# First loads of a decoder-layer kernel in another order, a separate buffer for the sample tokens, and query products in two groups of 64 columns

## The reference

```
mod = c @ w_ada + b_ada;  shift, scale, gate = split(mod, 3)
h = rmsnorm(x, g_norm) * (1 + scale) + shift
u = h @ w_in                       # queries, six k/v parts, gate logits, z_a, latents, z_b
y = [ NSA group * silu(z_a) | MLA group * silu(z_b) ]
x = x + gate * (y @ w_out);  then a final rmsnorm
```

## Time and profile before

| | |
|---|---|
| runs of the kernel before | 1237.3, 1240.06, 1241.99 us; median 1240.06 |
| the profiled execution | 1236.88 us |
| its span in the trace | 1235.1 us |
| mean granted clock of TensorE | 0.976 of full |
| busy: PE, DVE, ACT, POOL | 93%, 44%, 26%, 7% |
| first pass over the weights ends (L498 starts) | 231.9 us |

### The profile page before, as it was taken

How to read it: one execution, slowest core, us unless ns; L and a number is a source line. 1 busy time by engine, 2 the same in 40 slices (tenths; PEclk the granted TensorE clock), 3 DMA queues, 4 the chain that set the end, 5 groups by cost and what they waited for, 6 DMA issues and landing times.

```text
span 1235.1 us, 20092 instructions
## 1 busy us (share of the span) xinstructions
PE 1153.9 (93%) x7510; PEld 784.9 (64%) x7510; DVE 546.7 (44%) x1421; ACT 317.8 (26%) x636; POOL 86.6 (7%) x209
## 2 busy tenths in 40 slices
PE   6498999899999999998999999999999799999997
PEld 3265767544454667786878786865444466666665
DVE  0111211111111357776656564542333477777774
ACT  1111211110111256555434343431111122222220
POOL 0000000000000012111000000000000200000000
PEclk9698999999999999999999999999999899999997
DMA  9836220200000341000000000001982287666670
GB/s 344 221 111 226 61 94 9 88 7 4 6 4 7 69 111 51 2 1 1 1 1 2 1 2 1 2 1 67 169 285 71 84 294 249 228 224 224 214 198 20
DMA packets 91703, 115.89 MB, mean 94 GB/s; under 512 B 38513, under 2 KB 61476, under 8 KB 90584
## 3 DMA queue, kind: packets, MB, share of 16 engines
q1 hardware_dynamic: 91608, 114.61, 29.9%
HBM read 102.31 MB, written 12.27 MB: 93 GB/s over the span
## 4 chain that ended last, share of the span: by engine, by line
PE 74%; issue 9%; DVE 6%; ACT 5%; SPq 4%; DMA 2%; POOL 0%; ACTq 0%; POOLq 0%; DVEq 0%
PE PS L507 13%; PE PS L1583 9%; PE PS L1305 8%; PE PS L1336 6%; PE PS L1286 6%; PE PS L459 4%; PE PS L484 4%; ACT AR L1356 4%; PE PS L1275 3%; PE PS L1974 3%; PE PS L474 2%; PE PS L1939 2%; DMA AR<-in_x_prompt 2%; PE PS L1987 2%; PE PS L1282 2%
## 5 line engine op out<-in xcount | busy, mean ns | idle before, releaser
L1305 PE MATMUL PS<-AR 128*128 128x65 f32 (+1 forms) x1344 | 173.3, 269 | 0.9 <-DVE AR L1476 0.9
L1305 PEld LDWEIGHTS PS<-AR 128*128 128x128 f32 x1344 | 165.0, 192 | 1.3 <-issue 1.3
L507 PE MATMUL PS<-AR 128*128 128x512 f32 (+1 forms) x384 | 159.6, 575 | 2.7 <-DVE AR L755 2.7
L1356 ACT ACTIVATE AR<-PS,SM_ 128x64 f32<-128x64 f32 (+8 forms) x224 | 121.3, 594 | 54.4 <-PE PS L1336 36.2
L507 PEld LDWEIGHTS PS<-AR 128*128 128x128 f32 x384 | 72.3, 190 | 84.9 <-issue 81.2
L1336 PE MATMUL PS<-CA,AR 128*128 128x128 f32 x704 | 115.8, 280 | 0.2 <-ACT AR L1356 0.2
L1583 PE MATMUL PS<-AR 128*128 128x512 f32 x256 | 111.7, 592 | 0.0
L1393 DVE TENSOR_REDUCE SM_<-PS 128x2 f32<-128x512 f32 (+6 forms) x62 | 58.9, 950 | 114.3 <-PE PS L1286 62.3
L1336 PEld LDWEIGHTS PS<-CA,AR 128*128 128x128 f32 x704 | 80.3, 148 | 30.2 <-issue 15.6
L1366 ACT ACTIVATE AR<-PS 128x512 f32<-128x512 f32 (+1 forms) x108 | 59.1, 547 | 152.6 <-PE PS L1336 152.0
L1286 PE MATMUL PS<-AR 64*128 64x128 f32 (+3 forms) x512 | 74.3, 409 | 10.8 <-ACT AR L1356 10.2
(11 more groups left out here) (337 smaller groups left out, 1358.5 us busy)
## 6 DMA issues: line engine op xcount, KB each, us to landing
AR<-in_cache_nsa SPq DMA_DIRECT2D x128, 256.0 KB, 5.1
AR<-in_cache_mla SPq DMA_DIRECT2D x128, 96.0 KB, 4.2
AR<-in_x_prompt SPq DMA_DIRECT2D x16, 512.0 KB, 5.0
AR<-in_w_ada SPq DMA_DIRECT2D x3, 2048.0 KB, 15.7
AR<-in_w_in SPq DMA_DIRECT2D x1, 5888.0 KB, 17.7
out<-AR SPq DMA_DIRECT2D x9, 512.0 KB, 3.0
AR<-in_w_ada SPq DMA_DIRECT2D x8, 512.0 KB, 4.0
AR<-in_w_out SPq DMA_DIRECT2D x4, 1024.0 KB, 9.7
```

The lines of the kernel that those rows point to most:

```text
L507: mm = pe.matmul(PS[0:n, bank, 0:hi - lo], ht(j, k)[:, 0:n], w2cols(k, lo, hi), start=(k == 0), stop=(k == KT - 1))
L1305: mm = pe.matmul(out, tile, v, start=(n == 0), stop=(n == nb - 1))
L1356: act.activation(PB[:, o:o + n], PSF[:, o:o + n], ACT.Exp, bias=NM[:, u % 2, gi:gi + 1], scale=-1.0).then_inc(s_exp, 1)
```

## The change

It does five things.

1. The sample tokens get a buffer of their own (`XSS`), so `XS[0]` and `XS[1]` hold prompt tiles 1 and 2, tile j+2 goes into the buffer of tile j only for j from 1 to 6, and the loads have three semaphores.
2. SP's first loads stand in another order: `w_ada` as three loads of two k and two of one k, four of the six bias rows, tile 1, `W1` columns 512 to 1303 in one load, the query weights in one load, tile 2, the relative-bias table, the first two `ADAG`. The two last bias rows, three constant tables and the page table are loaded in round 1, after x of tile 3. In round 0 SP issues no x load.
3. The query weights are loaded as they lie in memory, 2 KB per row (before: 16 loads that reorder heads, 256 bytes a piece).
4. The prompt queries are products of 64 weight columns, group 0 to PSUM partitions 0 to 63 and group 1 to 64 to 127: twice as many products as before, each with the same 128 tokens. The sample queries read the same columns as the moving operand in two runs of 64.
5. In PE's rounds A comes first, and the transposes of tile j+1 and the gate pair stand behind A (in round 1 behind the sample queries and sample keys too). The transposes of tile 0 stand ahead of step 6 of the modulation, whose result goes to bank 7. ACT and DVE square and scale tile 2 at the end of round 0, behind the copies of the sample tokens' A and B.

```
@@ sp_projection
-            sp.dma_start(ADA[0], ada_v[:, 0, 0:2048]).then_inc(s_ada[0], 16)
...
-            for k in range(KT):
-                for g in range(G):
-                    sp.dma_start(W1[:, k, 0:512].rearrange("p (r g d) -> p r g d", r=R, g=G)[:, :, g, :],
-                                 w_in2[:, k, 256 * g:256 * g + 256].rearrange("p (r d) -> p r d", r=R))\
-                        .then_inc(s_w1q, 16)
...
+            sp.dma_start(XS[0], x_t[1]).then_inc(s_x[1], 16)
+            sp.dma_start(W1[:, :, 512:W1N], w_in2[:, :, 512:W1N]).then_inc(s_w1, 16)
+            sp.dma_start(W1[:, :, 0:512], w_in2[:, :, 0:512]).then_inc(s_w1q, 16)
+            sp.dma_start(XS[1], x_t[2]).then_inc(s_x[2], 16)
             sp.wait_ge(s_us, 1)
             sp.dma_start(U_dram, US[0:8, :]).then_inc(s_udma, 16)
             for j in IDX:
-                if j + 2 <= 8:
+                if 1 <= j <= 6:
                     sp.wait_ge(s_xt, j + 1)
-                    sp.dma_start(XS[j % 2], x_t[j + 2]).then_inc(s_x[j % 2], 16)
+                    sp.dma_start(xs(j + 2), x_t[j + 2]).then_inc(s_x[(j + 2) % 3], 16)
...
                 if j + 2 < KT:
                     sp.wait_ge(s_gk, 2 * j + 2)
@@ pe_projection
                 for r in range(R):
                     for k in range(KT):
-                        mm = pe.matmul(PS[:, 2, P * r:P * r + n], w1q(k, r), ht(j, k)[:, 0:n],
-                                       start=(k == 0), stop=(k == KT - 1))
+                        for g in range(G):
+                            mm = pe.matmul(PS[64 * g:64 * g + 64, 2, P * r:P * r + n], w1q(k, r, g), ht(j, k)[:, 0:n],
+                                           start=(k == 0), stop=(k == KT - 1))
```

More of the change, by code:

```diff
@@ L289, in ht, with xs @@
             return HTS[:, k, :] if j == 0 else HT[:, j - 1, k, :]
+        def xs(j):
+            return XSS if j == 0 else XS[(j - 1) % 2]
         def tok(j):
@@ L307, in z_mla, with w1q, w1q_both @@
             return ZNS[96:128, 0:512] if j == 0 else Z[:, j - 1, 512:1024]
-        def w1q(k, r):
-            return W1[:, k, P * r:P * r + P]
+        def w1q(k, r, g):
+            return W1[:, k, 256 * g + 64 * r:256 * g + 64 * r + 64]
+        def w1q_both(k, r):
+            return W1[:, k, 0:512].rearrange("p (g r d) -> p r g d", g=G, r=R)[:, r]
         def w2cols(k, lo, hi):
@@ L338, in sp_projection @@
-            sp.dma_start(W1[:, :, 512:1024], w_in2[:, :, 512:1024]).then_inc(s_w1, 16)
-            sp.dma_start(W1[:, :, 1024:W1N], w_in2[:, :, 1024:W1N]).then_inc(s_w1b, 16)
-            for k in range(KT):
-                for g in range(G):
-                    sp.dma_start(W1[:, k, 0:512].rearrange("p (r g d) -> p r g d", r=R, g=G)[:, :, g, :],
-                                 w_in2[:, k, 256 * g:256 * g + 256].rearrange("p (r d) -> p r d", r=R))\
-                        .then_inc(s_w1q, 16)
+            for n, base in enumerate((31360, 35456, 10432)):
+                sp.dma_start(view(base, 4096).rearrange("p (k n) -> p k n", k=2),
+                             ada_v[:, 2 * n:2 * n + 2, 0:2048]).then_inc(s_ada[n], 16)
+                if n == 0:
+                    sp.dma_start(RBA[0:32, :], rel_bias).then_inc(s_rb, 16)
+                    sp.dma_start(CB[0:33, :], cB).then_inc(s_rb, 16)
+                    sp.dma_start(GST[0:8, :], g_norm[0].rearrange("(k p) -> k p", p=P)).then_inc(s_rb, 16)
+                    sp.dma_start(GST[8:10, :], g_q_lat[0].rearrange("(k p) -> k p", p=P)).then_inc(s_rb, 16)
+                    sp.dma_start(XSS[0:RS, :], x_t[0]).then_inc(s_x[0], 16)
@@ new lines, in sp_projection @@
+            for k in (6, 7):
+                sp.dma_start(ADA[k], ada_v[:, k, 0:2048]).then_inc(s_ada[k - 3], 16)
+            for c in range(4):
+                sp.dma_start(BADA[32 * c:32 * c + 32, :], b_ada[:, 512 * c:512 * c + 512].to_broadcast([32, 512]))\
+                    .then_inc(s_bada, 16)
+            sp.dma_start(XS[0], x_t[1]).then_inc(s_x[1], 16)
+            sp.dma_start(W1[:, :, 512:W1N], w_in2[:, :, 512:W1N]).then_inc(s_w1, 16)
+            sp.dma_start(W1[:, :, 0:512], w_in2[:, :, 0:512]).then_inc(s_w1q, 16)
@@ new lines, in sp_projection @@
+                if j == 1:
+                    for c in (4, 5):
+                        sp.dma_start(BADG[32 * c - 128:32 * c - 96, :],
+                                     b_ada[:, 512 * c:512 * c + 512].to_broadcast([32, 512])).then_inc(s_bada, 16)
+                    sp.dma_start(CC[:], cC).then_inc(s_cst, 16)
+                    sp.dma_start(CD[:], cD).then_inc(s_cst, 16)
+                    sp.dma_start(CE[:], cE).then_inc(s_cst, 16)
+                    sp.dma_start(GKV, g_kv_lat.to_broadcast([P, P])).then_inc(s_cst, 16)
+                    sp.dma_start(PT_SB[:], page_table.rearrange("b n -> (b n)").rearrange("(a m) -> a m", a=1))\
+                        .then_inc(s_cst, 16)
@@ L411, in pe_projection @@
             for k in range(KT):
[L412 to L413 removed]
+                if k % 2 == 0 or k == 7:
+                    pe.wait_ge(s_ada[k // 2 if k < 6 else k - 3], 16)
+                if k == 6:
+                    pe.wait_ge(s_ctv, 4)
+                    pe_tokens(pe, 0)
                 for n in range(4):
[L415 removed]
+                    mm = pe.matmul(PS[32 * n:32 * n + 32, 7, :], CT[:, k, :], ADA[k][:, 512 * n:512 * n + 512],
                                    start=(k == 0), stop=(k == KT - 1))
@@ L452, in pe_projection @@
                     continue
[L453 to L456, removed]
                 pe.wait_ge(s_Ae, j)
@@ L470, in pe_projection @@
                     pe_keys(pe, 0)
+                if j < 8:
+                    pe_tokens(pe, j + 1)
+                pe.wait_ge(s_adag[(j - 1) % 2], 16 * ((j - 1) // 2 + 1))
+                for c in range(2):
+                    pe.matmul(PS[32 * c:32 * c + 32, 6, :], CT[:, j - 1, :], ADAG[(j - 1) % 2][:, 512 * c:512 * c + 512],
+                              start=(j == 1), stop=(j == KT)).then_inc(s_gk, 1)
                 pe.wait_ge(s_Be, j)
@@ L657, in act_squares @@
             junk = HT[0:n, (7, 6)[j] if j < 2 else j - 1, :, :].rearrange("p k t -> p (k t)")
-            act.activation(junk, XS[j % 2][0:n, :], ACT.Square, accum_out=SSQ[0:n, j:j + 1]).then_inc(s_ssq, 1)
+            act.activation(junk, xs(j)[0:n, :], ACT.Square, accum_out=SSQ[0:n, j:j + 1]).then_inc(s_ssq, 1)
         def dve_projection(dve):
```

54 lines of the change are left out of this document (18 added, 36 removed).

## The result

| | before | changed |
|---|---|---|
| median of ten runs each | 1239.85 us | 1250.97 us |
| lowest and highest | 1237.3, 1242.2 | 1245.1, 1256.3 |
| profiled execution (its span) | 1236.88 (1235.1) | 1246.68 (1244.9) |
| first pass over the weights ends | 231.9 | 239.3 |

The changed kernel is slower: 1.0085 of before, 95% interval 1.0069 to 1.0102. In a second set on another occasion it was 1.0101 (1.0086 to 1.0117). The forecast was 1248 (+8.1 us), the range 1242 to 1256.

What follows compares the result with a forecast made beforehand. PE, busy 93% of the span, was taken as the bound. Terms: +1.4 us to the keys of tile 2, +2.5 in round 3, +3.6 in round 4, +0.5 for Q, about +8.1: 1248 from a 1240.06 median; 8-in-10 range 1242 to 1256.

Steps and rivals of the forecast that it cites:

- the four waits: PE idle in rounds 1 to 4: 8.1 us at the sample queries, 12.4 before keys of tile 2, then 2.4 and 3.5.
- wait at the sample queries: Round 1: PE waits 8.1 us at the sample queries' transpose, until DVE has scaled tile 3 and copied them out.
- keys of tile 2: Round 2: keys start at 110.3 us, +1.4, behind `W2` and x of tile 4; PE stands 12.4 us instead of 5.4.
- wait before the keys of tile 3: Round 3: B and Q end 10.9 us behind the gate pair, DVE's copy 13.3 behind it: a stall of 2.4 us.
- wait before the keys of tile 4: Round 4: DVE's copy comes 14.4 us behind the gate pair, against 10.9 of B and Q: a stall of 3.5 us.
- Q in pairs, a round: Prompt queries as 128 products of 64 columns: 0 to 0.95 us more a tile, taken as 0.1, 0.5 in sum.
- Up to T1: Front to the end of round 1's gate pair: fed by memory, ending at 56.1 us, 6.9 earlier, bounds 55.0 to 58.
- The flights of x: Rounds 1 to 4: gate pair to release stays as before, 11.9, 23.3, 13.3 and 14.4 us for tiles 3 to 6.
- The early gain stays: Rival, 6%: x comes soon enough for B and Q to hide it; the pass ends 9 us sooner, 1231 us.
- column pairs that don't run at once: Rival on Q, 5%: at row pairs' speed 4.8 us instead of 0.5, 1252; fully one behind the other 1291 (2%).
- the clock behind the short waits: Rounds 3 and 4: neither short stall need cost clock, taken as nothing; +2.3 us each if it falls.
- slower by clock: Rival, 14%: the clock falls behind both short stalls in rounds 3 and 4, +4.6 us, giving 1253.

Runs made afterwards that it cites:

- the kernel with early x: Changed kernel, SP issuing x of tile 3 once tile 1 is transposed and later x right behind gate pairs, ahead of other weights: 1217.81 us, 0.982; again 1216.93 us.
- tiles 5 and 6 ahead: Changed kernel with x of tiles 5 and 6 issued ahead of the compression weights of its round: 1243.22 us, 1.0019 of before.
- the modulation ahead: The kernel with early x, with the modulation's bias and tables ahead of tile 1's scaling on DVE, and ACT's bias-row copy ahead of its squares: 1218.82 us, 0.9817.
- tile 3 early: Changed kernel with x of tile 3 alone issued once tile 1 is transposed, ahead of the wait for the first gate pair: 1240.67 us, 1.0008 of before.

## Why the prediction was right, and where it was off

The direction, the four waits and their places were right. How near the +7.4 of the first pass came to the forecast is partly luck, and the clock was priced too low. Step by step:

| step | forecast | measured |
|---|---|---|
| round-0 products start | 39.4 | 38.4 |
| first gate pair ends (T1) | 56.1 | 56.0 |
| wait at the sample queries | 8.1 | 6.9 |
| second gate pair ends (T2) | 87.0 | 86.2 |
| keys of tile 2 | 110.3 | 110.8 |
| third gate pair ends (T3) | 122.2 | 121.4 |
| wait before the keys of tile 3 | 2.4 | 2.0 |
| fourth gate pair ends (T4) | 144.8 | 143.6 |
| wait before the keys of tile 4 | 3.5 | 2.2 |
| Q in pairs, a round | +0.1 | +0.14 |
| first pass | +8.1 | +7.4 |
| time (median) | +8.1 | +11.1 |

- *Up to T1.* Right, partly by errors that cancel. I had the round-0 products wait for the weights until 39.4; they started at 38.4, right behind the transposes of tile 1 and with no wait (in three other traces with these loads the weights released them at 37.5 to 37.7). They took 5.7 us instead of 4.9, as their first part ran at half clock (granted 0.50 from 38 to 42). The tables (L434) took 3.9 us instead of 6.6, part of the distance of 9.9 that I had read from before (6.6 again in two other traces with this front), so the steps of the modulation ended at 28.7, not 33. It brought nothing: DVE stood on x of tile 1 and came to the bias at 32.6.
- *The flights of x.* The distances from gate pair to release were read from before. They came out 1.1, 0.2 and 1.1 us shorter for tiles 3, 5 and 6 (10.9 to the release, 13.1 behind T3, 13.3 behind T4), and 1.3 longer for tile 4 behind `W2` (24.6 against 23.3). For tile 3 the flight itself was shorter, 3.7 us against 4.7, and 3.4 to 3.7 in all four traces with this wait; for tile 6 SP needed 1.2 us less to issue the compression weights. The flight of tile 4 behind `W2` took 18.5 to 20.5 us in the eight traces that have one, so its distance can't be read from a single trace to better than 2 us.
- *The first pass* was forecast at +8.1 (the terms add up to 8.0) and measured at +7.4, but not by the same terms. The keys of tile 4 came at 156.9, +5.3 where I had +7.6: the keys of tiles 3 and 4 followed their gate pairs by 0.2 and 1.1 us less, and the way from the keys of tile 2 to T3 took 10.5 us and not 11.9, as the clock behind the long wait cost 1.2 us here, and 2.4 in three other traces. The slow A behind the keys of tile 4, which I had left out, gave 1.7 back, and Q the 0.5. That these nearly cancel is luck.
- *The early gain stays* (6%) was the rival that the kernel with early x then made true, by another order of issue: it is 22 us faster than before. It was right to give it little for this change, since the issue order behind the gate pair was not altered. The rival of column pairs that don't run at once fell with the 7.21 us.
- *The step that was mis-sized* is the clock behind the short waits. I took it as nothing in the forecast because 2.7 us of idleness had left the clock at 1.00. The changed kernel's windows (columns as in rows 5, the granted clock third from the end) show otherwise, behind 2.2 us and behind that same wait of 2.7 us at the start of the second pass:

```profile
157.00:159.00 2.00, 2.00 (x6) 1.01 (x6) 0.67 (x3) 0.49 (x2) 0.00 (x0) 0.76 0.00 0
159.00:161.00 2.00, 2.00 (x3) 0.79 (x3) 0.00 (x0) 0.00 (x0) 0.00 (x0) 0.50 0.00 0
249.00:251.00 2.00, 1.96 (x4) 1.01 (x5) 1.38 (x2) 0.00 (x0) 0.00 (x0) 0.80 0.06 16
251.00:253.00 2.00, 2.00 (x4) 1.00 (x3) 0.00 (x0) 0.00 (x0) 0.00 (x0) 0.50 0.00 0
```

Each time 1.7 us are lost (8.73 against 7.03 for A; 21.71 against 20.01 for 48 products). The first is in the +7.4 of the first pass; the second makes +9.1, and 0.7 more comes in attention and decode: the span's +9.8. The second trace of the changed kernel has two falls in the first pass (it ends at 241.8), one in the second, and a further 3.4 us in attention, where the granted clock was 0.98 of full in the first 98 us and had been 1.00: +14.8. Both are counted from the one trace of before, whose execution lies 3.0 us below its median; counted from that median they are +6.8 and +11.9, and the measured +11.1 lies between. How often the clock falls in the runs that were not traced is not shown. The rival "slower by clock" was half true in the first trace (one of the two short waits) and true in the second, so 14% was too low; neither it nor the forecast had the second pass, where the change does nothing.

## What to carry to other kernels

Before work is moved on the engine that bounds, ask which load flies under it. The trace of before gives, for each load, the time from the event that lets it go (here the gate pair) to the instruction that PE waits for (here 11.9, 23.3, 13.3 and 14.4 us), and the work between the two must stay longer than that. Fix the issue first: a load whose buffer is free should not stand behind a wait for something else, nor behind a large transfer that is not needed until later. In this kernel the new order of PE's rounds then cost nothing, and the gain at the front stayed a gain: 1217 to 1218 us against 1240.

A short wait on TensorE, here of 2.0 to 2.7 us, should be priced with both outcomes of the clock: its length alone, and its length plus 1.7 us.

## What the runs showed of the hardware

One and the same wait, the 2.68 to 2.69 us before the first full products of the second pass, stands in all twelve traces of this case. In the kernel before it is

```profile
241.62 20.01 PE L507 MATMUL PS<-AR 128*128 128x448 f32 x48 [2.69 <-DVE AR L755]
```

against the 21.71 us of the changed kernel (249.04, in the first listing). The 48 products behind it took 20.01 us in five (before, A ahead in the kernel before, tiles 5 and 6 ahead, the modulation ahead, the second run of early x) and 21.71 us in seven (changed, the changed kernel again, PE in the old order, early x, early x with the old order, tile 3 early, 64 columns in the kernel before). Neither the length of the wait nor the instructions around it tell them apart. In the first pass waits of 1.53, 1.97, 2.04 and 2.66 us left the clock at 1.00, and waits of 2.02, 2.12, 2.20 and 2.63 us did not. What decides it, no run here tells. Nor does the number of short waits tell how far the runs lie apart: ten runs of the changed kernel lay 11 us apart and five others 3.4; ten with tile 3 early 10.6 and ten with tiles 5 and 6 ahead 6.0; those of the kernel with early x, without such waits in the first pass, 4.7 and 1.4, but with PE in the old order, and one wait of 3.6 us, 13.3.
